# Scaling half of the causal attentions' probabilities on GpSimd, and copying a quarter of their turned blocks on VectorE

## What is computed

```python
def masked_softmax(s, mask):
    s = where(mask, s, -1e30); m = max(s); e = exp(s - m) * mask
    return e / maximum(sum(e), 1e-30)

# layer 0, "mla": 12 heads, q and k of width 96, v of width 64, causal
p = masked_softmax(q @ k.T * scale, key_pos <= query_pos);  o = p @ v
# layer 1, "nsa": 12 heads in 2 groups, three branches, each causal with an ALiBi bias
o = gate0 * o_compressed + gate1 * o_selected + gate2 * o_window
# both layers: 4 further heads over 256 memory tokens, no mask
p = softmax(q_mem @ k_mem.T * scale);  o_mem = p @ v_mem
```

## Time and profile before

| | |
|---|---|
| median of 3 runs | 3335.41 us (3335.27 to 3336.45) |
| the profiled execution, its own time | 3336.93 us |
| its span, first to last instruction | 3335.1 us |
| mean granted TensorE clock | 0.949 of full speed |
| busy share of the span: PE, PEld, DVE, ACT, POOL | 93%, 78%, 39%, 31%, 4% |
| mla attention | from 1689 to 1773 us of the span |
| nsa attention | from 2744 to 2897 us of the span |

### The profile page before, as it was taken

The page is one execution under the profiler, slowest core; times in us unless marked ns, Lnnn a source line. Parts: engine busy times, 40 slices in busy tenths (PEclk is TensorE's granted clock), DMA queues, the critical chain, the costliest instruction groups (busy, mean ns, idle before and its releaser), DMA issues.

```text
span 3335.1 us, 36129 instructions
## 1 busy us (share of the span) xinstructions
PE 3113.2 (93%) x15234; PEld 2588.6 (78%) x15234; DVE 1301.8 (39%) x1839; ACT 1048.8 (31%) x1808; POOL 142.6 (4%) x210
## 2 busy tenths in 40 slices
PE   7799989999999889999798999989999878889998
PEld 6688877889998878887666888878888754578886
DVE  3254334222232633332565333152332448653334
ACT  3123234323333422221373222112221127522221
POOL 1000010020000100000100000010000100000000
PEclk8899989978889899999899999999999979999999
DMA  6832222212222222322200332243233320022321
GB/s 184 178 101 90 100 89 73 76 56 76 70 76 70 70 76 89 101 97 89 90 25 26 114 101 89 101 103 114 91 99 101 104 69 1 14 88 89 101 95 70
DMA packets 136673, 287.33 MB, mean 86 GB/s; under 512 B 20378, under 2 KB 33050, under 8 KB 136384
## 3 DMA queue, kind: packets, MB, share of 16 engines
q1 hardware_dynamic: 125232, 247.17, 22.8%
q0 software_dynamic: 11280, 37.85, 5.0%
HBM read 271.30 MB, written 11.53 MB: 85 GB/s over the span
## 4 chain that ended last, share of the span: by engine, by line
PE 82%; DVE 10%; ACT 3%; issue 2%; DMA 2%; POOL 2%; DVEq 0%; POOLq 0%; ACTq 0%
PE bank L494 23%; PE bank L495 23%; PE bank L496 23%; PE bank L618 3%; PE bank L635 2%; DVE w_low L1307 1%; PE bank L650 1%; DMA raw<-in_a_w_in 1%; PE bank L626 1%; PE bank L669 1%; DVE small L1345 1%; DVE row L1343 1%; POOL small L1770 1%; DVE x_rows L1365 1%; PE bank L510 1%
## 5 line engine op out<-in xcount | busy, mean ns | idle before, releaser
L1307 DVE TENSOR_TENSOR w_low<-raw,w_high 128x2048 fp32r<-128x2048 f32 x235 | 531.1, 2260 | 1434.0 <-ACT w_high L980 1427.9
L980 ACT ACTIVATE w_high<-raw 128x2048 fp32r<-128x2048 f32 x235 | 443.6, 1888 | 1184.8 <-PE bank L496 1059.3
L494 PE MATMUL bank<-xt_high,w_high 128*128 128x512 f32 (+1 forms) x2060 | 806.0, 391 | 3.2 <-DVE w_low L1307 2.7
L495 PE MATMUL bank<-xt_low,w_high 128*128 128x512 f32 (+1 forms) x2060 | 803.9, 390 | 0.0
L496 PE MATMUL bank<-xt_high,w_low 128*128 128x512 f32 (+1 forms) x2060 | 803.7, 390 | 0.0
L494 PEld LDWEIGHTS bank<-xt_high,w_high 128*128 128x128 f32 (+1 forms) x2060 | 388.0, 188 | 84.6 <-DVE w_low L1307 3.3
L496 PEld LDWEIGHTS bank<-xt_high,w_low 128*128 128x128 f32 (+1 forms) x2060 | 387.5, 188 | 82.1
L495 PEld LDWEIGHTS bank<-xt_low,w_high 128*128 128x128 f32 (+1 forms) x2060 | 387.9, 188 | 80.3
L494 PE MATMUL bank<-w_high,hidden_high 128*128 128x512 f32 x704 | 275.5, 391 | 9.8 <-DVE w_low L1307 6.7
L496 PE MATMUL bank<-w_high,hidden_low 128*128 128x512 f32 x704 | 274.0, 389 | 0.0
L495 PE MATMUL bank<-w_low,hidden_high 128*128 128x512 f32 x704 | 274.0, 389 | 0.0
(11 more groups left out here) (310 smaller groups left out, 3680.9 us busy)
## 6 DMA issues: line engine op xcount, KB each, us to landing
raw<-in_ffn_w_gu SPq DMA_DIRECT2D x80, 1024.0 KB, 5.1
raw<-in_ffn_w_down SPq DMA_DIRECT2D x44, 1024.0 KB, 5.0
raw<-in_b_w_in SPq DMA_DIRECT2D x40, 1024.0 KB, 5.1
raw<-in_a_w_in SPq DMA_DIRECT2D x24, 1024.0 KB, 5.2
raw<-in_a_w_out SPq DMA_DIRECT2D x8, 1024.0 KB, 5.0
raw<-in_ffn_w_gu SPq DMA_DIRECT2D x16, 512.0 KB, 4.6
raw<-in_w_out SPq DMA_DIRECT2D x5, 1024.0 KB, 4.9
raw<-in_w_mem_kv SPq DMA_DIRECT2D x4, 1024.0 KB, 9.6
```

What stands on the lines that cost most here:

```text
L494: pe.matmul(o, lh, rh, start=start, stop=False, skip_group_check=True)
L495: pe.matmul(o, lh, rl, start=False, stop=False, skip_group_check=True)
L980: act.activation(WH[n % 2][:, 0:w], RAW[n % 2][:, 0:w], ACT.Copy).then_inc(sem["w_high_ready"], step("w_high_ready", n))
L1307: dve.tensor_tensor(WL[n % 2][:, 0:w], RAW[n % 2][:, 0:w], WH[n % 2][:, 0:w].bitcast(F32), ALU.subtract).then_inc(sem["w_low_ready"], step ...
```

## The change

Tasks with an odd number are scaled on GpSimd in place of VectorE. VectorE still computes every reciprocal; behind that of an odd task it no longer waits, but signals `sum_inverted`, and GpSimd's new loop `scale_pairs` scales the row in place. The turned blocks of tasks with `m % 4 == 2` are copied by VectorE, in its step m+5, in place of ScalarE in its step m+4. TensorE waits for the semaphore of whichever engine did the work; ahead of the products with v it now waits for the copies of both tasks.

```diff
+    def copier(m):
+        return "pt_copied_dve" if m % 4 == 2 else "pt_copied"
...
@@ TensorE, attend_pairs
                     for m in (2 * u - 4, 2 * u - 3):
-                        pe.wait_ge(sem["p_scaled"], at("p_scaled", (name, m)))
+                        scaled = "p_scaled_pool" if m % 2 else "p_scaled"
+                        pe.wait_ge(sem[scaled], at(scaled, (name, m)))
                         if m >= 2:
-                            pe.wait_ge(sem["pt_copied"], at("pt_copied", (name, m - 2)))
+                            copied = copier(m - 2)
+                            pe.wait_ge(sem[copied], at(copied, (name, m - 2)))
...
                     a, b = 2 * u - 6, 2 * u - 5
-                    pe.wait_ge(sem["pt_copied"], at("pt_copied", (name, b)))
+                    for m in (a, b):
+                        copied = copier(m)
+                        pe.wait_ge(sem[copied], at(copied, (name, m)))
...
@@ ScalarE, attend_pairs
-                if 4 <= n < N + 4:
+                if 4 <= n < N + 4 and copier(n - 4) == "pt_copied":
...
@@ VectorE, attend_pairs
-                    link(dve.reciprocal(rd, DS[:, m % 8:m % 8 + 1]))
-                    if tk["finish"] is not None:
+                    ins = dve.reciprocal(rd, DS[:, m % 8:m % 8 + 1])
+                    if m % 2:
+                        ins.then_inc(sem["sum_inverted"], step("sum_inverted", (name, m)))
+                    else:
+                        link(ins)
+                    if m % 2:
+                        pass
+                    elif tk["finish"] is not None:
...
+                if 5 <= n < N + 5 and copier(n - 5) == "pt_copied_dve":
+                    m = n - 5
+                    dve.wait_ge(sem["p_turned"], at("p_turned", (name, m)))
+                    if m >= 4:
+                        dve.wait_ge(sem["weighted"], at("weighted", (name, m - 4)))
+                    w = P * len(tasks[m]["turns"])
+                    dve.tensor_copy(PTs[m % 4][:, 0:w], ps[4 + m % 2][:, 0:w]).then_inc(sem["pt_copied_dve"], step("pt_copied_dve", (name, m)))
...
@@ GpSimd, called in front of rows("l01") and of rows("l11")
+        def scale_pairs(name):
+
+            tasks, SBs, _ = ATT[name]
+            for m in range(1, len(tasks), 2):
+                tk = tasks[m]
+                pool.wait_ge(sem["sum_inverted"], at("sum_inverted", (name, m)))
+                sb, rd = tk["view"](SBs[m % 6]), RD[:, m % 8:m % 8 + 1]
+                if tk["finish"] is not None:
+                    ins = pool.tensor_scalar(sb, sb, rd, tk["finish"], ALU.mult, ALU.mult)
+                else:
+                    ins = pool.tensor_scalar(sb, sb, rd, None, ALU.mult)
+                ins.then_inc(sem["p_scaled_pool"], step("p_scaled_pool", (name, m)))
```

More of the change, by code:

```diff
@@ L101 @@
     x_loaded3 xt_ready y_high_ready y_multiplied y_split p_scaled
-    pair_done pair_high pair_split pair_summed cmp_v_spread gates_turned gates_t_read
+    pair_done pair_high pair_split pair_summed sum_inverted p_scaled_pool pt_copied_dve cmp_v_spread gates_turned gates_t_read
 """
@@ L1865, in _ @@
         gains("l01", *GAINS["l01"])
+        scale_pairs("mla")
         rows("l01")
@@ L1899, in _ @@
         gains("l11", *GAINS["l11"])
+        scale_pairs("nsa")
         rows("l11")
```

## The result

The changed kernel takes 3342.6 us (median of 18 runs, 3337.39 to 3346.65), the kernel before, run on the same chip, 3335.6 us (18 runs, 3331.55 to 3338.25). The ratio is 1.0022, with an interval of 1.0015 to 1.0029: 7.0 us slower, and 5.0 to 9.7 by the interval. The interval lies across the 0.2% line between "the same" and "slower"; the time is inside the range, and the loss is three times the +2.2 us of the sum.

The account below looks back on a forecast made before the run. TensorE was taken to bound mla, a chain of waits between engines nsa. Terms -0.7 + 2.25 + 0.7 = +2.2 us gave a predicted median of 3337.6 us; the range leaving out 2 in 10 was 3331 to 3346.

Parts of the forecast that it names:

- GpSimd's price: Scalings put on GpSimd: 0.8 us for 512 columns, 0.5 us for 256, with bounds of 0.55 and 0.97 for 512.
- The last task of an mla pair: Mla, last task's turning: with GpSimd's scaling ready at 1721.28 against about 1721.25 before, 0 us, no slack.
- the slower rival: GpSimd's scaling becomes the late one: 1.5 us for 512 columns, +15.7 us, 3351.1 us; chance 0.19.
- Bias tables: Between nsa pairs, GpSimd's scaling of task 13 makes VectorE's bias tables start 0.45 us late: +2.25 us over 5 boundaries.
- Scalings taken off VectorE: Both attentions: a gain only ahead of the pair's sum in nsa, 0.12 us for each of 6 pairs, -0.7 us.
- Copies taken off ScalarE: Both attentions, 16 and 28 copies: none of the copies waited for is among them, so 0 gain on the path.
- Turning of task 15: End of an nsa pair: with GpSimd's scaling ready at 2813.44 against a start at 2813.42, 0 us, no slack left.
- TensorE's additional waits: Ahead of the products, 30 and 54 steps wait for a second copy: 0 us.
- Last task of each attention: End of each attention: reciprocal to turning takes 0.80 us with GpSimd, 0.45 before; +0.35 us twice, +0.7 us.
- The sign that the text had set for being wrong: Both attentions: the prediction is wrong if turnings wait for GpSimd by more than some 5 us in all.
- The other sign: Nsa window: the prediction is wrong if TensorE's idle time falls below 20 us.
- The relief rival: Relief of VectorE and ScalarE halves the 23.6 us that turnings wait for copies: 3323.6 us; chance 0.11.

Follow-up runs that it names:

- the form is mended: The changed kernel with GpSimd's one-operation scaling given a second multiplication by 1.0: 3335.04 us against 3335.72 for the kernel before, ratio 0.9998.
- the copies alone: The change without its first part: VectorE makes every scaling as before and every fourth copy; 3347.86 us in one execution.
- the run with the even tasks: Against the kernel before, GpSimd scales the even tasks (two-operation form), VectorE the odd ones, ScalarE makes all copies; 3330.3 us in one execution.

## Why the prediction was right or wrong

*GpSimd's price, "I take 0.8 us for 512, 0.5 us for 256".* This is the step of the prediction that failed. One price stood for two forms of the instruction, and I had not looked at the second operation. For the two-operation form it was good: 0.77 and 0.55 us. For the one-operation form it was 1.56 and 0.92 us, outside the upper bound of 0.97 for 512, and all of mla uses that form.

*"The last task of an mla pair ... 0, again with no slack".* It failed by its price, and named one place of two. A middle pair of mla is 0.67 us longer than before (11.55 against 10.88 from one pair's first turning to the next): about 0.35 us arise at the turning of task 5, the 384-wide one, where the sum had no term, and 0.3 at the last task. At 1.5 us the slower rival, which names both widths, gave mla +5.7 us and 0.7 more for its end; measured are +5.1 us with the end, and 4.5 of them go when the form is mended. That rival was right for mla and wrong for nsa, where it put +9.3 us on the border and on task 15. The Trainium skill (GPSIMD Engine Reference, "Key points"), with VectorE about twice as fast, fits neither form: 0.77 against 0.55 us in nsa is 1.4 times, 1.56 against 0.48 us in mla more than three times.

*"Bias tables ... +0.45 us at each of 5 boundaries".* The hold is there, 0.35 us each time, but a pair is 21.69 us long where it was 21.73. The starts of the masks behind the tables show where the hold is won back. The eighth mask of a pair is still 0.35 us late (10.12 against 9.77 us), the ninth 0.09 us (11.32 against 11.23), the next tables 0.04 us early. So 0.26 us are gained ahead of the pair's sum, where the forecast had 0.12, and 0.13 ahead of the tables, where it had set scaling and copy as equal, 0.55 against 0.546 us. Where VectorE scaled task 13, the hold was gone, but that brought back a scaling that costs 0.25 us more than the hold. Of the +2.6 us that nsa's window shows, 0.8 us are its memory tasks in the one-operation form, and 1.6 us its last pair, which took 23.27 us. There the granted clock fell to 0.50 for 3.4 us, which it doesn't in the trace with the two-operation form (1.00 throughout, 21.71 us for that pair). The stretch behind the fall, beside the one ahead of it:

```profile
2814.00:2836.00 22.00, 18.53 (x154) 11.04 (x155) 17.39 (x67) 14.81 (x46) 4.86 (x8) 1.00 0.00 1
2836.00:2858.00 22.00, 18.93 (x149) 11.18 (x147) 16.17 (x61) 13.33 (x43) 4.32 (x8) 0.92 0.00 1
```

*"Scalings taken off VectorE ... -0.7 us".* Too small: alone they gained 1.9 us in nsa's causal tasks, copies left out. The reason given, that the even scaling stays in front of the last exponential and the odd one stands behind it, is what the run with the even tasks shows: nsa's causal tasks 7.0 us shorter than before.

*"Copies taken off ScalarE ... Gain on the path: 0".* That none of the waited-for copies leaves ScalarE was right (15.1 us of waits remain of 18.8). That they cost VectorE nothing, since "nothing but VectorE's next mask is queued behind them", was wrong: at two of four places the next mask or the tables are just what the chain waits for, and beside all scalings the copies cost 0.66 us a pair at the full clock, beside the even ones 2.0 us in the stage. It did not show in the result because the odd scalings left at the same time.

*"Turning of task 15 ... 0".* Right: it starts 0.24 us behind task 14's, released by ScalarE. *"TensorE's additional waits ... 0".* Right for the products, which wait for no copy in the rows. But the turnings that use a bank freed by VectorE do, 2.3 us in mla with the form mended, and the stage is 0.5 us longer than before; the prediction had them in front of a later turning anyway. *"Last task of each attention ... +0.35 us, twice".* With two operations the memory tasks are 0.35 and 0.2 us longer; with one, 1.6 and 0.8.

The sign that the text had set for being wrong, turnings that wait for GpSimd by more than some 5 us, was met: 6.2 us in mla and 2.3 in nsa. The other sign, less than 20 us of idle time in nsa, was not (25.1 us). The range held, and the class as far as an interval across its line can tell, but that was in part luck: mla's loss alone was more than twice the sum, by a term that the sum had at 0, and in nsa a gain of 2 us and a cost of 2 us cancelled each other, neither of which the sum had at its size. *The relief rival* had a mechanism that exists (turnings wait for copies 7.8 in place of 18.8 us once VectorE's chain is shorter), for an edit other than this one.

## What to carry to other kernels

Ask of each instruction that is moved off an engine what stands directly behind it in that engine's order: here the even scalings, in front of a mask that others wait for, were worth 9 us in the two stages, and the odd ones, behind it, 2. Price each form of an instruction apart (here by the number of its operations), since the one with less to do may be the slower. When a change has two halves, run each alone: a total near zero was plus two and minus two here. And read the granted clock of a stage before its length is put down to the edit: of the 10.7 us of the copies alone, some 6 went with the clock.

## What the runs showed of the hardware that was not expected

- GpSimd's tensor_scalar on float32 with one operation takes 603, 924, 1242 and 1563 ns for 128, 256, 384 and 512 columns, 2.5 ns a column. With a second multiplication by a constant it takes 372, 480, 586 and 693 ns, 0.84 ns a column and 0.27 us beside, and with two operands from SBUF 447, 554, 662 and 769 ns, 0.84 ns a column again. Why the form with one operation is slower was not tried and stays open.
- VectorE with two inputs in SBUF and GpSimd hold each other up, and the order decides who pays: with GpSimd 0.27 us ahead the tables took 0.35 us more, with the tables 0.19 us ahead GpSimd took 2.45 us in place of 0.77. The Trainium skill (SBUF - State Buffer, "Who interferes with whom") says that whoever issues first has the shared ports for its whole instruction and the other is blocked. The order agrees both times; the length does not quite, since the tables lost 0.35 of the 0.50 us that GpSimd's row still ran.
- VectorE's scalings are held at some places and not at others. In nsa the five of 128x128 that start 0.21 us behind a 512-wide scaling on GpSimd took 638 ns, the other seven 346. In mla, with the one-operation form on GpSimd, five of six 512-wide ones start 0.54 us behind GpSimd's, run wholly beside it and take the 487 ns of before. There GpSimd, which started first, is the longer one, 1386 ns against the 1242 of the sixth time, so that rule does not hold for them, and the measurement decides:

```profile
1719.91 1.39 POOL L1805 TENSOR_SCALAR m_p<-m_p,small 128x384 f32<-128x384 f32 x1 [2.35 <-DVE small L1451]
1720.45 0.49 DVE L1461 TENSOR_SCALAR m_p<-m_p,small 128x512 f32<-128x512 f32 x1
```

  The sixth of them started 0.82 us behind GpSimd's and took 702 ns. What decides which of the two is held was not tried and stays open.
